# A hybrid decoder trunk: block attention with its transposes two heads back, the gated branch at even heads, weight rests one turn ahead

## The chip, the cores and the metric

One core of a Trainium2 chip runs the whole program. The metric is the time of one execution in microseconds on the device. The engines are TensorE (PE), VectorE (DVE), ScalarE (ACT), GpSimd (POOL) and SyncE (SP). Each works through its own program in order, and waits on semaphores for the others.

## What is computed

Two layers of a decoder trunk on 256 tokens of width 1024, float32. Each layer has a mixer of three branches, a cross-attention and a feed-forward part (dense in the first layer, 8 experts in the second). The part that matters here is the mixer's first two branches:

```python
y_a = moba_attention(q_m, k_m, v_m) @ w_up_moba[l]      # 8 heads of 64, causal, one block of 256
y_s = gelu(s5_ssm(u_s, ...))
glu_a, glu_b = split(y_s @ ssm_w_glu[l], 2)
y_b = glu_a * sigmoid(glu_b)
merged = sigmoid(gate_a) * y_a + sigmoid(gate_b) * y_b + sigmoid(gate_c) * y_c
```

With 256 tokens and blocks of 256 there is no past block, so `moba_attention` is causal softmax attention for each head.

## The kernel before

Tokens lie in two tiles of 128 partitions. The program is written by hand for every engine: each engine's block runs once over the layers, and the order of the work is the order of the Python code there. Products with precision beyond one pass use a split of both operands in a high part and a rest; ScalarE copies the high part of a weight group (`unit_split_hi`, L988), VectorE subtracts it (`unit_split_lo`, L1519), and `split_out` (L2409, L2410, L2413) multiplies low by high, high by high and high by low.

The attention stage of a layer mixes two kinds of work on TensorE. Its loop `for s in range(MH + 2)` does in turn s: the scores of head s (`m_scores`, L2587 and L2588), one half of a gated product of the second branch (`glu_half`, 12 products of 512 columns), the transposes of head s-1 (`m_tr`, L2597) and the output of head s-2 (`m_out`, L2608 to L2610). Two halves make one gated product, four products a stage. Behind the loop `up(U_UPM, ...)` projects the attention's output with the same `split_out` lines, on `m_hi` and `m_lo`.

For each head VectorE adds the causal mask and takes the row maxima (`moba_max`, L1765 to L1768), ScalarE takes exp (`moba_exp`, L1144 and L1146), VectorE divides by the row sums (`moba_norm`, L1774 to L1776), TensorE transposes, and ScalarE copies the transposed weights out of PSUM (`moba_pT`, L1154). For each gated product ScalarE takes tanh (`glu_tanh`, L1164), and VectorE works the branch out (`glu_branch`, L1782, L1785, L1786); the next gated product waits for its first instruction, which frees bank 0. For each pair of heads ScalarE copies the output's high part (`moba_oT`, L1158) and VectorE takes the rest (`moba_lo`, L1756). In between VectorE makes eight weight rests (L1519) of the next units.

VectorE's order is:

```python
moba_max(0)
for h in range(MH):
    if h + 1 < MH: moba_max(h + 1)
    moba_norm(h)
    if h % 2 == 1: glu_branch(h // 2)
    unit_split_lo(...)                       # one weight rest
    if h >= 3 and h % 2 == 1: moba_lo((h - 3) // 2)
moba_lo(MH // 2 - 1)
```

The probability buffers `mp_` are two, used by heads in turn, and the maxima, negated maxima and sums (`mx`, `nm`, `rs`) two columns for each. Behind the stage ScalarE goes on with the first taps of a convolution (`first_taps`, L1191), VectorE with the other taps (L1822) and `moba_branch` (L1833), which takes the projection.

## Time and profile before

| | us |
|---|---|
| three runs: median (lowest, highest) | 1891.79 (1882.14, 1892.0) |
| the profiled execution, its own time | 1885.03 |
| its span, first to last instruction | 1883.3 |
| TensorE busy | 1787.7 (95%) |
| VectorE busy | 1394.2 (74%) |
| ScalarE busy | 1044.9 (55%) |
| mean granted TensorE clock | 0.982 |
| attention stage, first layer | 222.0 to 266.4 |
| attention stage, second layer | 844.9 to 889.3 |

A stage is counted from its first scores to the start of the projection behind it. A granted clock of 1 is 2.4 GHz, of 0.5 is 1.2 GHz. Matmul records overlap, so a wait of TensorE is read from the brackets of a row, which give the idle time before it and what ended it.

### The profile page before, as it was taken

The numbers are of one execution on the slowest core, as the hardware profiler recorded it, in microseconds if no ns is written. First come the engines' busy times: TensorE is split into PE (matmuls) and PEld (weight loads), VectorE is DVE, ScalarE is ACT, GpSimd is POOL, SyncE is SP. The second block draws the span as 40 slices with busy tenths as digits, with TensorE's granted clock in tenths as the row PEclk, the third lists the DMA queues.
The fourth block names the chain that finished last, engine by engine and source line by source line (L and its number), as shares of the span: only waits on it lengthen the run. The fifth ranks groups of instructions, "written<-read, shape, count | busy, mean of one in ns | idle before, by whom it ended". The sixth has DMA issues, their size and how long they took to land.

```text
span 1883.3 us, 23760 instructions
## 1 busy us (share of the span) xinstructions
PE 1787.7 (95%) x9559; PEld 1421.6 (75%) x9559; DVE 1394.2 (74%) x1742; ACT 1044.9 (55%) x1208; POOL 171.9 (9%) x229
## 2 busy tenths in 40 slices
PE   7999999998999999999999889999999999999995
PEld 5787766576888788776657678787878787878784
DVE  5688678445555478867844478989898989989895
ACT  4234555345444422455523657767676767777773
POOL 8420002010000324000200010000000000000010
PEclk9999999999999999999999989999999999999998
DMA  7334431066552433543204469999999999999992
GB/s 248 135 135 155 158 111 69 1 247 236 176 200 89 155 131 135 179 164 105 90 1 163 174 252 390 379 389 361 389 359 389 362 389 360 390 358 390 347 391 84
DMA packets 204572, 434.93 MB, mean 231 GB/s; under 512 B 6888, under 2 KB 45936, under 8 KB 204464
## 3 DMA queue, kind: packets, MB, share of 16 engines
q1 hardware_dynamic: 196464, 414.20, 60.8%
q0 software_dynamic: 5136, 17.01, 2.5%
q10 hardware_dynamic: 2864, 2.23, 0.4%
q8 instruction: 73, 1.20, 0.3%
q14 instruction: 35, 0.29, 0.0%
HBM read 422.93 MB, written 10.49 MB: 230 GB/s over the span
## 4 chain that ended last, share of the span: by engine, by line
PE 79%; DVE 11%; ACT 6%; issue 3%; DMA 1%; ACTq 0%; POOL 0%; DVEq 0%; SPq 0%
PE bank L2855 14%; PE bank L2857 14%; PE bank L2856 14%; PE bank L2467 4%; DVE split_e L1525 3%; PE bank L2487 3%; PE bank L2491 3%; PE bank L2488 3%; PE bank L2409 2%; PE bank L2386 2%; PE bank L2413 2%; PE bank L2410 2%; PE bank L2393 2%; PE bank L2658 1%; DVE ring_r L1519 1%
## 5 line engine op out<-in xcount | busy, mean ns | idle before, releaser
L1525 DVE TENSOR_TENSOR split_e<-ring,split_e 128x2048 fp32r<-128x2048 f32 x264 | 600.3, 2288 | 51.0 <-ACT split_e L999 50.8
L999 ACT ACTIVATE split_e<-ring 128x2048 fp32r<-128x2048 f32 x264 | 503.8, 1919 | 160.7 <-PE bank L2857 157.1
L2855 PE MATMUL bank<-split_e,fx_e 128*128 128x512 f32 x704 | 278.8, 396 | 2.0 <-DVE fx_e L2246 2.0
L2857 PE MATMUL bank<-split_e,fx_e 128*128 128x512 f32 x704 | 274.7, 390 | 0.0
L2856 PE MATMUL bank<-split_e,fx_e 128*128 128x512 f32 x704 | 274.2, 389 | 0.0
L2855 PEld LDWEIGHTS bank<-split_e,fx_e 128*128 128x128 f32 x704 | 132.2, 188 | 28.2 <-DVE fx_e L2246 2.2
L2857 PEld LDWEIGHTS bank<-split_e,fx_e 128*128 128x128 f32 x704 | 132.1, 188 | 28.2
L2856 PEld LDWEIGHTS bank<-split_e,fx_e 128*128 128x128 f32 x704 | 132.4, 188 | 26.2
L2855 PE MATMUL bank<-split_e,f_actT_e 128*128 128x512 f32 x352 | 138.7, 394 | 9.2 <-DVE f_actT_e L2254 9.2
L2857 PE MATMUL bank<-split_e,f_actT_e 128*128 128x512 f32 x352 | 137.1, 389 | 0.0
L2856 PE MATMUL bank<-split_e,f_actT_e 128*128 128x512 f32 x352 | 137.1, 389 | 0.0
L988 ACT ACTIVATE ring_r<-ring 128x1024 fp32r<-128x1024 f32 x71 | 73.5, 1056 | 71.4 <-PE bank L2488 57.0
L1519 DVE TENSOR_TENSOR ring_r<-ring,ring_r 128x1024 fp32r<-128x1024 f32 x71 | 86.7, 1251 | 29.7 <-ACT ring_r L988 29.4
L2855 PEld LDWEIGHTS bank<-split_e,f_actT_e 128*128 128x128 f32 x352 | 66.1, 188 | 26.1 <-DVE f_actT_e L2254 12.8
L2467 PE MATMUL bank<-hT,ring 128*128 128x256 f32 x384 | 84.5, 381 | 0.0
L2467 PEld LDWEIGHTS bank<-hT,ring 128*128 128x128 f32 x384 | 72.5, 190 | 10.3
L2857 PEld LDWEIGHTS bank<-split_e,f_actT_e 128*128 128x128 f32 x352 | 66.1, 188 | 13.9
L2856 PEld LDWEIGHTS bank<-split_e,f_actT_e 128*128 128x128 f32 x352 | 66.1, 188 | 13.3
L2855 PE MATMUL bank<-split_mix,fx 128*128 128x512 f32 x168 | 66.5, 396 | 1.7 <-DVE phase L2189 1.7
L2857 PE MATMUL bank<-split_mix,fx 128*128 128x512 f32 x168 | 65.5, 390 | 0.0
L2856 PE MATMUL bank<-split_mix,fx 128*128 128x512 f32 x168 | 65.4, 389 | 0.0
L988 ACT ACTIVATE phase_r<-ring 128x1024 fp32r<-128x1024 f32 x34 | 35.7, 1057 | 46.4 <-PE bank L2488 46.4
(598 smaller groups left out, 3404.8 us busy)
## 6 DMA issues: line engine op xcount, KB each, us to landing
ring<-in_moe_w_gate SPq DMA_DIRECT2D x40, 2048.0 KB, 11.5
ring<-in_moe_w_up SPq DMA_DIRECT2D x40, 2048.0 KB, 11.5
ring<-in_moe_w_down SPq DMA_DIRECT2D x40, 2048.0 KB, 11.5
ring<-in_w_in SPq DMA_DIRECT2D x28, 2048.0 KB, 8.0
ring<-in_ffn_w_gate SPq DMA_DIRECT2D x11, 1024.0 KB, 5.5
ring<-in_ffn_w_up SPq DMA_DIRECT2D x11, 1024.0 KB, 8.0
ring<-in_ffn_w_down SPq DMA_DIRECT2D x11, 1024.0 KB, 8.8
ring<-in_ssm_w_glu SPq DMA_DIRECT2D x8, 1024.0 KB, 6.2
```

Source lines behind the costliest of these rows:

```text
L988: nc.scalar.activation(unit_hi(l, m), unit_raw(j, i), ACT.Copy).then_inc(split_hi, 1)
L999: nc.scalar.activation(split_e[j % NBUF][:, HI, :], ring[:, s * PIECE + i * HGRP:s * PIECE + (i + 1) * HGRP], ACT.Copy).then_inc(split_hi, 1)
L1519: V.tensor_tensor(unit_lo(j, i), unit_raw(j, i), unit_hi(l, m).bitcast(F32), ALU.subtract).then_inc(split_lo, 1)
L1525: V.tensor_tensor(split_e[j % NBUF][:, LO, :], ring[:, s * PIECE + i * HGRP:s * PIECE + (i + 1) * HGRP], split_e[j % NBUF][:, HI, :].bitca ...
L2386: last = mm(B[banks[m // 2]][:, (m % 2) * SEQ:(m % 2 + 1) * SEQ], w[:, k, m * P:(m + 1) * P], src[:, k, :], start=k == 0, stop=k == KD - 1)
L2467: last = mm(B[t][:, (m % 2) * SEQ:(m % 2 + 1) * SEQ], w[:, k, m * P:(m + 1) * P], hT[:, k, :], start=k == 0, stop=k == KD - 1)
L2487: mm(bank[:, :], h_lo[:, k, at], hi, start=k == 0, stop=False)
L2488: freed = mm(bank[:, :], h_hi(k)[:, at], hi, start=False, stop=False)
L2491: last = mm(bank[:, :], h_hi(k)[:, at], lo, start=False, stop=k == KD - 1)
L2855: mm(bank, a[HI], w[HI], start=first, stop=False)
L2856: mm(bank, a[HI], w[LO], start=False, stop=False)
L2857: return mm(bank, a[LO], w[HI], start=False, stop=last_one)
```

## The change

The three engines' programs of the attention stage are rewritten:

- TensorE's loop has one more turn. The transposes in turn s are those of head s-2, the output is that of head s-3. Scores and gated halves stay where they were.
- `mp_` has a third buffer, heads use them in turn by `h % 3`, and the maxima and sums have columns of their own (`m_mx`, `m_nm`, `m_rs`).
- ScalarE's copies of transposed weights follow: head s-2 in turn s, the output's high part at even turns from 4.
- VectorE takes the maxima two heads ahead, does the gated branch at even heads h, right behind the normalisation of head h, and has one weight rest between the first two maxima, with the others one turn ahead. `moba_lo` comes at even h from 4, the last two behind the loop.

```diff
--- before.py
+++ after.py
@@ -253,6 +253,8 @@
         glu_t = [rm.take(512) for _ in range(2)]
         glu_y = [rm.take(512) for _ in range(2)]
         gl_tmp = [rm.take(512) for _ in range(2)]
+        mp_.append(rm.take(3 * P))
+        m_mx, m_nm, m_rs = (st[:, 32 + 8 * i:38 + 8 * i] for i in range(3))
 
 
         rg = Region(phase, PH)
@@ -1139,12 +1141,12 @@
                 def moba_exp(h):
                     n = MH * l + h
                     act.wait_ge(ms_neg, n + 1)
-                    p = mp_[h % 2]
-                    o = 2 * (h % 2)
-                    nc.scalar.activation(p[:, 0:P], p[:, 0:P], ACT.Exp, bias=nm[:, o:o + 1], scale=MD ** -0.5,
-                                         accum_out=rs[:, o:o + 1])
-                    nc.scalar.activation(p[:, P:3 * P], p[:, P:3 * P], ACT.Exp, bias=nm[:, o + 1:o + 2],
-                                         scale=MD ** -0.5, accum_out=rs[:, o + 1:o + 2]).then_inc(ms_exp, 1)
+                    p = mp_[h % 3]
+                    o = 2 * (h % 3)
+                    nc.scalar.activation(p[:, 0:P], p[:, 0:P], ACT.Exp, bias=m_nm[:, o:o + 1], scale=MD ** -0.5,
+                                         accum_out=m_rs[:, o:o + 1])
+                    nc.scalar.activation(p[:, P:3 * P], p[:, P:3 * P], ACT.Exp, bias=m_nm[:, o + 1:o + 2],
+                                         scale=MD ** -0.5, accum_out=m_rs[:, o + 1:o + 2]).then_inc(ms_exp, 1)
 
                 def moba_pT(h):
                     n = MH * l + h
@@ -1163,19 +1165,19 @@
                         act.wait_ge(glu_used, 4 * l + i - 1)
                     nc.scalar.activation(glu_t[i % 2], B[1][:, :], ACT.Tanh, scale=0.5).then_inc(glu_th, 1)
 
-                for s in range(MH + 2):
+                for s in range(MH + 3):
                     if s < MH:
                         moba_exp(s)
                     if 2 <= s <= MH and s % 2 == 0:
                         glu_tanh(s // 2 - 1)
                     if 5 <= s <= 8:
                         unit_split_hi(l, U_UPM, [s - 5])
-                    if 1 <= s <= MH:
-                        moba_pT(s - 1)
+                    if 2 <= s <= MH + 1:
+                        moba_pT(s - 2)
                     if s < 2:
                         unit_split_hi(l, U_GLU + 1, [2 + s])
-                    if s >= 3 and s % 2 == 1:
-                        moba_oT((s - 3) // 2)
+                    if s >= 4 and s % 2 == 0:
+                        moba_oT((s - 4) // 2)
 
                 def keys_copy(b):
                     act.wait_ge(xk_ps, 6 * l + b + 1)
@@ -1758,22 +1760,24 @@
 
                 def moba_max(h):
                     n = MH * l + h
-                    p, o = mp_[h % 2], 2 * (h % 2)
+                    p, o = mp_[h % 3], 2 * (h % 3)
                     dve.wait_ge(ms_ready, n + 1)
-                    if n >= 2:
-                        dve.wait_ge(ms_tr, n - 1)
+                    if h >= 3:
+                        dve.wait_ge(ms_tr, n - 2)
+                    elif l > 0:
+                        dve.wait_ge(ms_tr, MH * l)
                     link(V.tensor_tensor(p, B[2 + h % 2][:, 0:3 * P], causal[:, :], ALU.add))
-                    V.tensor_reduce(mx[:, o:o + 1], p[:, 0:P], AX.X, ALU.max)
-                    link(V.tensor_reduce(mx[:, o + 1:o + 2], p[:, P:3 * P], AX.X, ALU.max))
-                    V.tensor_scalar(nm[:, o:o + 2], mx[:, o:o + 2], -MD ** -0.5, None, ALU.mult).then_inc(ms_neg, 1)
+                    V.tensor_reduce(m_mx[:, o:o + 1], p[:, 0:P], AX.X, ALU.max)
+                    link(V.tensor_reduce(m_mx[:, o + 1:o + 2], p[:, P:3 * P], AX.X, ALU.max))
+                    V.tensor_scalar(m_nm[:, o:o + 2], m_mx[:, o:o + 2], -MD ** -0.5, None, ALU.mult).then_inc(ms_neg, 1)
 
                 def moba_norm(h):
                     n = MH * l + h
-                    p, o = mp_[h % 2], 2 * (h % 2)
+                    p, o = mp_[h % 3], 2 * (h % 3)
                     dve.wait_ge(ms_exp, n + 1)
-                    link(V.reciprocal(rs[:, o:o + 2], rs[:, o:o + 2]))
-                    V.tensor_scalar(p[:, 0:P], p[:, 0:P], rs[:, o:o + 1], None, ALU.mult)
-                    V.tensor_scalar(p[:, P:3 * P], p[:, P:3 * P], rs[:, o + 1:o + 2], None, ALU.mult).then_inc(ms_norm, 1)
+                    link(V.reciprocal(m_rs[:, o:o + 2], m_rs[:, o:o + 2]))
+                    V.tensor_scalar(p[:, 0:P], p[:, 0:P], m_rs[:, o:o + 1], None, ALU.mult)
+                    V.tensor_scalar(p[:, P:3 * P], p[:, P:3 * P], m_rs[:, o + 1:o + 2], None, ALU.mult).then_inc(ms_norm, 1)
 
 
                 def glu_branch(i):
@@ -1789,19 +1793,22 @@
                     dve.wait_ge(consts, 4)
                 dve.wait_ge(mtr_ready, 4 * (l + 1))
                 moba_max(0)
+                unit_split_lo(l, U_GLU + 1, [0])
+                moba_max(1)
                 for h in range(MH):
-                    if h + 1 < MH:
-                        moba_max(h + 1)
+                    if h + 2 < MH:
+                        moba_max(h + 2)
                     moba_norm(h)
-                    if h % 2 == 1:
+                    if h % 2 == 0:
                         glu_branch(h // 2)
-                    if h < 4:
-                        unit_split_lo(l, U_GLU + 1, [h])
-                    if 4 <= h:
-                        unit_split_lo(l, U_UPM, [h - 4])
-                    if h >= 3 and h % 2 == 1:
-                        moba_lo((h - 3) // 2)
-                moba_lo(MH // 2 - 1)
+                    if h < 3:
+                        unit_split_lo(l, U_GLU + 1, [h + 1])
+                    elif h < 7:
+                        unit_split_lo(l, U_UPM, [h - 3])
+                    if h >= 4 and h % 2 == 0:
+                        moba_lo((h - 4) // 2)
+                for j in range(MH // 2 - 2, MH // 2):
+                    moba_lo(j)
 
                 ab4 = ab.rearrange("p (t c h) -> p t c h", t=NT, c=2)
                 z4 = gate_z.rearrange("p (t h) -> p t h", t=NT)
@@ -2594,7 +2601,7 @@
                     if h >= 2:
                         pe.wait_ge(ms_pT, n - 1)
                     for b in range(3):
-                        last = tr(B[4 + h % 2][:, b * P:(b + 1) * P], mp_[h % 2][:, b * P:(b + 1) * P], ident[:, :])
+                        last = tr(B[4 + h % 2][:, b * P:(b + 1) * P], mp_[h % 3][:, b * P:(b + 1) * P], ident[:, :])
                     last.then_inc(ms_tr, 1)
 
                 def m_out(h):
@@ -2622,15 +2629,15 @@
                     if half == 1:
                         last.then_inc(glu_ps, 1)
 
-                for s in range(MH + 2):
+                for s in range(MH + 3):
                     if s < MH:
                         m_scores(s)
                     if 1 <= s <= MH:
                         glu_half((s - 1) // 2, (s - 1) % 2)
-                    if 1 <= s <= MH:
-                        m_tr(s - 1)
-                    if s >= 2:
-                        m_out(s - 2)
+                    if 2 <= s <= MH + 1:
+                        m_tr(s - 2)
+                    if s >= 3:
+                        m_out(s - 3)
 
                 def up(j, src, n, src_ready, turns=range(4)):
                     for i in turns:
```

**VectorE, from the first gated branch to the next normalisation** (L1782 to L1786 are the branch, L1519 a weight rest, L1765 to L1768 the maximum, L1774 to L1776 the normalisation). Before:

```order
L1782 SCALAR_TENSOR_TENSOR phase<-phase,bank 128x512
L1785 SCALAR_TENSOR_TENSOR phase<-gates,phase 128x512
L1786 TENSOR_SCALAR qk<-phase 128x512
L1519 TENSOR_TENSOR ring_r<-ring,ring_r 128x1024
L1765 TENSOR_TENSOR phase<-bank,causal 128x384
L1766 TENSOR_REDUCE st<-phase 128x1
L1767 TENSOR_REDUCE st<-phase 128x1
L1768 TENSOR_SCALAR st<-st 128x2
L1774 RECIPROCAL st<-st 128x2
L1775 TENSOR_SCALAR phase<-phase,st 128x128
L1776 TENSOR_SCALAR phase<-phase,st 128x256
```

With the change:

```order
L1786 SCALAR_TENSOR_TENSOR phase<-phase,bank 128x512
L1789 SCALAR_TENSOR_TENSOR phase<-gates,phase 128x512
L1790 TENSOR_SCALAR qk<-phase 128x512
L1521 TENSOR_TENSOR ring_r<-ring,ring_r 128x1024
L1769 TENSOR_TENSOR phase<-bank,causal 128x384
L1770 TENSOR_REDUCE st<-phase 128x1
L1771 TENSOR_REDUCE st<-phase 128x1
L1772 TENSOR_SCALAR st<-st 128x2
L1778 RECIPROCAL st<-st 128x2
L1779 TENSOR_SCALAR phase<-phase,st 128x128
L1780 TENSOR_SCALAR phase<-phase,st 128x256
```

The rows are the same but for line numbers; before, the last three normalise head 2, now head 1.

**VectorE, the end of the stage, in the last gated branch.** Before:

```order
L1774 RECIPROCAL st<-st 128x2
L1775 TENSOR_SCALAR phase<-phase,st 128x128
L1776 TENSOR_SCALAR phase<-phase,st 128x256
L1782 SCALAR_TENSOR_TENSOR phase<-phase,bank 128x512
L1785 SCALAR_TENSOR_TENSOR phase<-gates,phase 128x512
L1786 TENSOR_SCALAR qk<-phase 128x512
L1519 TENSOR_TENSOR ring_r<-ring,ring_r 128x1024
L1756 TENSOR_TENSOR m_lo<-bank,m_hi 128x256 x2
L1810 TENSOR_TENSOR st<-st,small_bc 128x4 x2
```

With the change:

```order
L1786 SCALAR_TENSOR_TENSOR phase<-phase,bank 128x512
L1789 SCALAR_TENSOR_TENSOR phase<-gates,phase 128x512
L1790 TENSOR_SCALAR qk<-phase 128x512
L1521 TENSOR_TENSOR ring_r<-ring,ring_r 128x1024
L1758 TENSOR_TENSOR m_lo<-bank,m_hi 128x256
L1778 RECIPROCAL st<-st 128x2
L1779 TENSOR_SCALAR phase<-phase,st 128x128
L1780 TENSOR_SCALAR phase<-phase,st 128x256
L1758 TENSOR_TENSOR m_lo<-bank,m_hi 128x256 x2
L1817 TENSOR_TENSOR st<-st,small_bc 128x4 x2
```

The normalisation of head 7 has moved from ahead of the branch to behind it and its weight rest. An L1756 that followed the third branch now stands ahead of that normalisation; the last two L1756 stay last.

**TensorE, the end of the stage, from the last gated product on** (L2597 are transposes, L2608 to L2610 an output; L2604 and L2615 to L2617 with the change). Before:

```order
L2413 MATMUL bank<-ring_r,y_hi 128x512
L2597 MATMUL bank<-ident,phase 128x128 x3
L2608 MATMUL bank<-phase,v_tok 64x128
L2609 MATMUL bank<-phase,v_tok 64x128
L2610 MATMUL bank<-phase,v_tok 64x128
L2608 MATMUL bank<-phase,v_tok 64x128
L2609 MATMUL bank<-phase,v_tok 64x128
L2610 MATMUL bank<-phase,v_tok 64x128
L2409 MATMUL bank<-ring_r,m_lo 128x512
```

With the change:

```order
L2420 MATMUL bank<-ring_r,y_hi 128x512
L2604 MATMUL bank<-ident,phase 128x128 x3
L2615 MATMUL bank<-phase,v_tok 64x128
L2616 MATMUL bank<-phase,v_tok 64x128
L2617 MATMUL bank<-phase,v_tok 64x128
L2604 MATMUL bank<-ident,phase 128x128 x3
L2615 MATMUL bank<-phase,v_tok 64x128
L2616 MATMUL bank<-phase,v_tok 64x128
L2617 MATMUL bank<-phase,v_tok 64x128
L2615 MATMUL bank<-phase,v_tok 64x128
L2616 MATMUL bank<-phase,v_tok 64x128
L2617 MATMUL bank<-phase,v_tok 64x128
```

One output (of head 5) stands between the last gated product's transposes and those of head 7, and two outputs behind them, ahead of the projection.

## Rows read from the trace of the kernel before

**Rows 1.** The page's head and the shares of its chain by engine

```profile
span 1883.3 us, 23760 instructions
...
PE 79%; DVE 11%; ACT 6%; issue 3%; DMA 1%; ACTq 0%; POOL 0%; DVEq 0%; SPq 0%
```

**Rows 2.** Windows of the stage: us, busy PE, PEld, DVE, ACT, POOL, clock, DMA, GB/s

```profile
222.00:266.40 44.40, 39.71 (x201) 28.86 (x201) 31.71 (x78) 21.75 (x55) 1.17 (x2) 1.00 0.27 94
844.90:889.30 44.40, 39.67 (x200) 28.83 (x200) 31.69 (x78) 21.81 (x56) 1.17 (x2) 1.00 0.27 95
```

**Rows 3.** Timeline, TensorE: start us, us, engine, line, operation [idle before, releaser]

```profile
226.48 0.55 PE L2597 MATMUL bank<-ident,phase 128*128 128x128 f32 x3 [0.56 <-DVE phase L1776]
...
227.81 0.50 PE L2409 MATMUL bank<-ring_r,y_lo 128*128 128x512 f32 x1
...
236.65 0.55 PE L2597 MATMUL bank<-ident,phase 128*128 128x128 f32 x3 [0.86 <-DVE phase L1776]
...
247.95 0.55 PE L2597 MATMUL bank<-ident,phase 128*128 128x128 f32 x3 [1.19 <-DVE phase L1776]
...
259.25 0.55 PE L2597 MATMUL bank<-ident,phase 128*128 128x128 f32 x3 [1.19 <-DVE phase L1776]
```

**Rows 4.** Timeline, VectorE, a gated branch and what follows it, layer 0

```profile
231.50 0.69 DVE L1782 SCALAR_TENSOR_TENSOR phase<-phase,bank 128x512 f32<-128x512 f32 x1 [1.53 <-ACT phase L1164]
...
233.41 1.22 DVE L1519 TENSOR_TENSOR ring_r<-ring,ring_r 128x1024 fp32r<-128x1024 f32 x1
234.55 0.55 DVE L1765 TENSOR_TENSOR phase<-bank,causal 128x384 f32<-128x384 f32 x1
...
235.86 0.16 DVE L1774 RECIPROCAL st<-st 128x2 f32<-128x2 f32 x1
...
245.52 0.42 DVE L1756 TENSOR_TENSOR m_lo<-bank,m_hi 128x256 fp32r<-128x256 f32 x1
```

**Rows 5.** Timeline, VectorE, the last gated branch of the stage

```profile
264.23 0.69 DVE L1782 SCALAR_TENSOR_TENSOR phase<-phase,bank 128x512 f32<-128x512 f32 x1 [1.80 <-ACT phase L1164]
...
266.14 1.23 DVE L1519 TENSOR_TENSOR ring_r<-ring,ring_r 128x1024 fp32r<-128x1024 f32 x1
267.28 0.75 DVE L1756 TENSOR_TENSOR m_lo<-bank,m_hi 128x256 fp32r<-128x256 f32 x2
```

**Rows 6.** Timeline, TensorE, the end of the stage

```profile
263.41 0.49 PE L2597 MATMUL bank<-ident,phase 128*128 128x128 f32 x3
263.82 0.43 PE L2608 MATMUL bank<-phase,v_tok 128*64 128x128 f32 x2
...
265.58 0.43 PE L2608 MATMUL bank<-phase,v_tok 128*64 128x128 f32 x2 [0.88 <-ACT phase L1154]
...
266.38 0.50 PE L2409 MATMUL bank<-ring_r,m_lo 128*128 128x512 f32 x1
```

**Rows 7.** Timeline, ScalarE, the end of the stage

```profile
265.04 0.48 ACT L1154 ACTIVATE phase<-bank 128x384 f32<-128x384 f32 x1
266.48 0.39 ACT L1158 ACTIVATE m_hi<-bank 128x256 fp32r<-128x256 f32 x1 [0.96 <-PE bank L2610]
```

**Rows 8.** Chain that ended last, in order of time, behind the stage: start us, us, what

```profile
266.76 3.30 ACT phase L1191 x8
...
276.70 3.26 DVE phase L1822 x8
```

**Rows 9.** Timeline, TensorE, and windows of 1 us with the granted clock

```profile
287.99 5.40 PE L2672 MATMUL bank<-ring,ones 128*128 128x512 f32 x8 [2.73 <-ACT ring L1220]
...
289.00:290.00 1.00, 1.00 (x3) 0.44 (x2) 1.00 (x3) 1.00 (x3) 0.00 (x0) 0.71 0.00 0
290.00:291.00 1.00, 1.00 (x2) 0.34 (x1) 1.00 (x4) 0.98 (x2) 0.00 (x0) 0.50 0.00 0
291.00:292.00 1.00, 1.00 (x3) 0.43 (x2) 0.96 (x3) 0.99 (x3) 0.00 (x0) 0.50 0.00 0
292.00:293.00 1.00, 1.00 (x3) 0.47 (x2) 1.00 (x3) 1.00 (x3) 0.00 (x0) 0.59 0.00 0
```

## The prediction

> **What bounds the kernel now.** I read the page's head and chain first: a span of 1883.3 us, 79% of its chain on TensorE, only 11% on VectorE [rows 1]. The change is confined to the attention stage of the two layers. The windows of that stage show 44.4 us in each, TensorE busy for 39.7 of them, VectorE for 31.7 and ScalarE for 21.8, at the full granted clock [rows 2]. So no engine is full there: the loss is in hand-overs, and the order of waits decides. The two windows agree to 0.05 us of work, so I work the first layer out and count it twice.
>
> TensorE's timeline shows the hand-overs. It waits for the normalised weights of a head (released by VectorE's L1776) before the transposes of every second turn: 0.56, 0.86, 1.19 and 1.19 us [rows 3]. In the other turns it does not wait. Together that is 3.80 us a layer, and what the change could aim at.
>
> VectorE's timeline shows why every second turn. The gated branch starts when tanh is there (231.50). It holds VectorE to 233.41, the weight rest (L1519) to 234.55, the next head's mask and maximum to 235.86, and then the normalisation starts [rows 4]. The transposes start at 236.65 [rows 3]. From branch to transposes that is 1.91 + 1.14 + 1.31 + 0.79 = 5.15 us of VectorE's own in-order work. None of it is a wait for exp, and none a wait for another head's buffer. The 1.19 of the later turns is 0.33 more than 0.86: there the rest L1756 stands in the same row of work (its record alone is 0.42) [rows 3, 4].
>
> **The change, part by part.** A third probability buffer, their own statistics columns, and the altered waits of the maximum cost nothing by themselves: the same instructions run, and the buffers lie in space that is free at that time. What they could give is nothing either: the maximum never waited for a free buffer in the rows above.
>
> *TensorE transposes two heads back.* The transposes of head s-2 now stand where those of head s-1 stood. VectorE's program shifted along with them: between a gated branch and the transposes that wait for it there is still branch, weight rest, maximum, normalisation, only with a lower head number in the last. The order fences show it. So the 5.15 us stay, and with them the 0.86 waits. The extra head in flight is slack against exp, and exp is not what is late.
>
> *The start.* The first transposes leave the second turn: their wait of 0.56 goes, and they themselves (0.41, from 263.41 to 263.82 [rows 6]) move behind the second half of the gated product, which started at 227.81 [rows 3]. The first tanh, branch and everything chained to it come 0.56 + 0.41 = 0.97 us earlier. VectorE is ready for that: its rest, three maxima and normalisation take about 5.7 us by rows 4 from the first maximum, and the tanh comes after that. Gain: 0.97.
>
> *The L1756 rests come later.* The first of them leaves the second branch's row and goes to the third's, the second goes from the third to the last. So the wait behind the second branch falls from 1.19 to 0.86 [rows 3]: 0.33 gained. The third keeps its 1.19.
>
> *The weight rests one turn ahead.* The first now stands between the first two maxima. It delays the second maximum by 1.14, but its exp isn't needed before head 1 is normalised a turn later. Behind each gated branch there still stands exactly one rest. Cost and gain: nothing; should exp 1 be late after all, up to 1.14.
>
> *The end.* Here the shift has its price. Before, head 7 was normalised ahead of the last gated branch; its transposes and the output of head 6 ran at once (263.41, 263.82), the output of head 7 at 265.58 after ScalarE's copy of 265.04, and the next projection began at 266.38 [rows 6, 7]. That is 2.15 us behind the start of the last branch (264.23) [rows 5]. Now head 7's normalisation stands behind that branch, its weight rest and one L1756: 1.91 + 1.14 [rows 5] + 0.33, then 0.79 from normalisation to transposes [rows 3, 4], so the transposes start 4.17 behind the branch. Then they take 0.41, and the outputs of heads 6 and 7 0.80 each (265.58 to 266.38 [rows 6]); ScalarE's copy fits beside the first of these. The projection begins at 4.17 + 0.41 + 0.80 + 0.80 = 6.18. Loss: 6.18 - 2.15 = 4.03 us. TensorE stands idle for some 3.8 of it, from its output of head 5 (0.39 behind the branch's start) to 4.17.
>
> Is this loss covered by what follows? The chain behind the stage goes on with ScalarE's L1191 at 266.76, which stands in its program right behind the copy of head 7's output (266.48) [rows 7, 8]; that copy moves by the same 4.03. VectorE's next long piece, L1822 [rows 8], comes after a projection that moves by the same too. No engine has a start of its own there, so nothing is hidden.
>
> Sum for a layer: 4.03 - 0.97 - 0.33 = 2.73; for two 5.5 us.
>
> *TensorE's clock.* Behind a wait of 2.73 us the granted clock of this kernel fell to 0.71, 0.50, 0.50 and 0.59 in four successive microseconds, to its lower level (1.2 GHz) and back [rows 9]: 0.29 + 0.50 + 0.50 + 0.41 = 1.70 us of full-speed work lost. The stage itself, with waits of at most 1.19, kept 1.00 [rows 2, 3]. The new gap of 3.8 us is longer than the one of rows 9, so I expect a fall in each layer. If it lies inside the gap it costs nothing, if it lies on the transposes, outputs and projection, 1.70. I take the middle, 0.85 a layer, 1.7 us in all. The ends are 0 and 3.4. The Trainium skill (TensorE: Matmul & The Clock Gate, "Part 1: The HAM clock gate") says that TensorE drops to 1.2 GHz once it has been idle and gets 2.4 GHz back once it has been busy again. By that rule a fall is due in each layer, and the sum could be up to 5.5 + 3.4 = 8.9 (an estimate); by the stage's own rows, without a fall, it would be 5.5. Rows 9 agree with the rule, which speaks against this change.
>
> Forecast: 5.5 + 1.7 = 7.2 us slower. The profiled execution took 1885.03 by its own time, which gives 1892.2. But the three runs shown have their median at 1891.79 and their lowest at 1882.14, so executions of this kernel scatter by 10 us. The mean of all four is 1887.7; on it the changed kernel stands at 1895. About 0.5% (9.4 us) is what a measurement of this kernel can tell from no change, so the forecast is "no change", on the slow side.
>
> **Rivals.**
> *A, slower beyond 0.5%: TensorE stays at its lower clock.* Place: from the new gap through transposes and outputs (short bursts with little work) into the projection. If one fall follows another there, each at its 1.70 [rows 9], a layer loses 3.4 instead of 0.85, and the change 5.5 + 6.8 = 12.3 us: 1900 on the same mean (1897.3 on the profiled execution). It decides from the point where the second fall begins before the projection has run. For it: the gap is longer than in rows 9 and thin work follows. Against: in rows 9 the clock came back while work went on. The Trainium skill's rule above bears A out if those short bursts leave TensorE idle in its sense; no row shows that either way. Chance 0.16.
> *B, the pipeline does what its name says.* All waits of rows 3 vanish and the end is hidden: 3.80 a layer, 7.6 us, 1880 (1877.4 on the profiled execution). Against: the row of VectorE work between branch and transposes is the same by the order. Chance 0.08.
> *C, the end is taken up by the stage behind.* Then only 0.97 + 0.33 count: 2.6 us faster, 1885 (1882.4). For it: VectorE is busy there and waits little. Against: the chain starts that stage on ScalarE right behind the moved copy [rows 8]. Chance 0.10.
>
> **How the numbers follow.** Forecast 0.66, A 0.16, B 0.08, C 0.10. The range runs from C's 1885 to A's 1900, widened for the scatter of a median by 2 to 3 us, and leaves B and part of A out: 1883 to 1903. Slower by over 0.5%: three quarters of A (0.12), and a fifth of the forecast, whose 7.2 lies 2.2 below the bound (0.14), together 0.26. Faster by over 0.5%: half of B, helped by scatter, 0.04. The rest, 0.70, is no change.
>
> **What would show it.** In the changed profile each stage should show, on TensorE, no wait before the first transposes, then some 1.3 us before those of head 1 (the output that stood in this turn is gone, so TensorE is earlier there, while VectorE's 5.15 is the same), 0.86 before head 3, 1.19 before head 5, and a new wait of 3.7 to 3.8 before head 7, released by VectorE's normalisation (now L1780). The projection should begin 6.2 us behind the last branch, not 2.15, and the stage last 2.7 us longer at full clock, up to 6 us with falls. A lower clock should appear in the first microseconds around that wait. The forecast is wrong if the waits of heads 1, 3 and 5 vanish (B), if L1191 does not move against the last branch (C), or if the clock is below full for over 4 us in a layer (A).

## The result, and the profile after

The changed kernel takes 1889.63 us (median of 20 runs, 1887.14 to 1894.69), the kernel before 1884.8 us (20 runs, 1879.42 to 1892.0). The ratio is 1.0026, with a 95% interval of 1.0017 to 1.0035: the change makes the kernel slower by 4.9 us, between 3.2 and 6.6.

The page of the changed kernel, its head and the shares of its chain:

```profile
span 1887.1 us, 23759 instructions
...
PE 75%; DVE 14%; ACT 6%; issue 3%; DMA 1%; ACTq 0%; POOL 0%; DVEq 0%; SPq 0%
```

Against [rows 1] the span is 3.8 us longer, and 4% of the chain moved from TensorE to the others. The windows of the two stages, first scores to the projection, in the columns of [rows 2]:

```profile
223.20:271.10 47.90, 40.50 (x201) 29.56 (x201) 32.94 (x79) 21.84 (x55) 1.17 (x2) 0.97 0.33 124
848.00:895.90 47.90, 40.49 (x201) 29.57 (x201) 32.95 (x79) 21.88 (x55) 1.17 (x2) 0.97 0.35 123
```

A stage takes 47.9 us where it took 44.4 [rows 2]: 3.5 us more for the same instructions, and its mean clock is 0.97 where it was 1.00. TensorE's timeline, with the waits in brackets:

```profile
223.18 0.50 PE L2594 MATMUL bank<-phase 64*128 64x128 f32 x4 [0.98 <-ACT phase L1136]
...
230.81 0.38 PE L2604 MATMUL bank<-ident,phase 128*128 128x128 f32 x2
...
232.28 0.50 PE L2416 MATMUL bank<-ring_r,y_lo 128*128 128x512 f32 x1 [0.23 <-DVE phase L1786]
...
236.69 0.55 PE L2604 MATMUL bank<-ident,phase 128*128 128x128 f32 x3 [1.39 <-DVE phase L1780]
...
247.66 0.55 PE L2604 MATMUL bank<-ident,phase 128*128 128x128 f32 x3 [0.86 <-DVE phase L1780]
...
258.97 0.55 PE L2604 MATMUL bank<-ident,phase 128*128 128x128 f32 x3 [1.20 <-DVE phase L1780]
...
263.54 0.43 PE L2615 MATMUL bank<-phase,v_tok 128*64 128x128 f32 x2
...
268.13 0.90 PE L2604 MATMUL bank<-ident,phase 128*128 128x128 f32 x3 [3.72 <-DVE phase L1780]
268.96 0.69 PE L2615 MATMUL bank<-phase,v_tok 128*64 128x128 f32 x2
...
271.08 0.72 PE L2416 MATMUL bank<-ring_r,m_lo 128*128 128x512 f32 x1
```

These rows answer to [rows 3, 6]. The wait of 0.56 before the first transposes is gone (230.81, no bracket). Those of every second turn are there: 1.39, 0.86 and 1.20, and a small one of 0.23 before a gated product. New is the wait of 3.72 before the last transposes, which VectorE's L1780 ends, the normalisation of head 7. From those transposes (268.13) to the projection (271.08) it is 2.95 us. VectorE's side, first and last gated branch:

```profile
231.53 0.69 DVE L1786 SCALAR_TENSOR_TENSOR phase<-phase,bank 128x512 f32<-128x512 f32 x1 [1.49 <-ACT phase L1166]
...
263.95 0.69 DVE L1786 SCALAR_TENSOR_TENSOR phase<-phase,bank 128x512 f32<-128x512 f32 x1 [1.80 <-ACT phase L1166]
...
265.86 1.23 DVE L1521 TENSOR_TENSOR ring_r<-ring,ring_r 128x1024 fp32r<-128x1024 f32 x1
267.00 0.42 DVE L1758 TENSOR_TENSOR m_lo<-bank,m_hi 128x256 fp32r<-128x256 f32 x1
267.34 0.16 DVE L1778 RECIPROCAL st<-st 128x2 f32<-128x2 f32 x1
```

The first branch starts 8.35 us behind the first scores (223.18), where it was 9.50 (222.00 to 231.50). Behind the last one (263.95) stand the weight rest, an L1758 and only then the normalisation (267.34); the transposes start 4.18 us behind the branch. ScalarE, in answer to [rows 7, 8]:

```profile
271.19 0.38 ACT L1160 ACTIVATE m_hi<-bank 128x256 fp32r<-128x256 f32 x1 [1.63 <-PE bank L2617]
271.47 3.29 ACT L1193 ACTIVATE phase<-phase,params 128x256 f32<-128x256 f32 x8
```

It starts on L1193 (before: L1191) 0.28 us behind its copy of the last output, as before, and the chain goes on from there. The windows of 1 us around the last transposes:

```profile
267.00:268.00 1.00, 0.00 (x0) 0.00 (x0) 0.96 (x6) 0.00 (x0) 0.00 (x0) 1.00 0.97 369
268.00:269.00 1.00, 0.87 (x4) 0.54 (x4) 0.41 (x2) 0.00 (x0) 0.00 (x0) 0.58 1.06 408
269.00:270.00 1.00, 1.00 (x8) 1.00 (x9) 0.00 (x0) 0.49 (x1) 0.00 (x0) 0.50 1.02 389
270.00:271.00 1.00, 1.00 (x9) 0.75 (x5) 0.00 (x0) 0.00 (x0) 0.00 (x0) 0.50 0.85 330
271.00:272.00 1.00, 1.00 (x4) 0.82 (x4) 0.39 (x2) 0.81 (x3) 0.00 (x0) 0.71 0.13 49
272.00:273.00 1.00, 1.00 (x6) 0.81 (x5) 0.34 (x4) 1.00 (x3) 0.00 (x0) 1.00 0.00 0
```

In the gap TensorE's clock was still granted in full; at 268 it fell to the lower level and came back before 272. Adding up what each microsecond lacks to 1.00, that loses 0.42 + 0.50 + 0.50 + 0.29 = 1.71 us of full-speed work, the size of the fall in [rows 9]. The fall of [rows 9] itself, at 289, has no counterpart here. The wait that came ahead of it is there:

```profile
292.69 3.70 PE L2679 MATMUL bank<-ring,ones 128*128 128x512 f32 x8 [2.63 <-ACT ring L1222]
```

but the products behind it start at full clock:

```profile
293.00:294.00 1.00, 1.00 (x3) 0.38 (x2) 0.96 (x4) 1.00 (x3) 0.00 (x0) 1.00 0.00 0
```

The first products of the loop behind them, in the first layer, before and after:

```profile
306.35 1.37 PE L2719 MATMUL bank<-uT,ring 64*64 64x64 f32 x32 [0.43 <-POOL ring L876]
...
309.42 1.36 PE L2726 MATMUL bank<-uT,ring 64*64 64x64 f32 x32 [0.49 <-POOL ring L878]
```

From these sums of squares (287.99 in [rows 9], 292.69 here) to the loop (L2719 before, L2726 after) the profile of before has 18.4 and 18.2 us in its two layers, that of after 16.7 in both. So the profiled executions differ by 2 x 3.52 in the stages, less 1.63 and 1.47 behind them: 3.9, where the span differs by 3.8. Elsewhere they differ too, but the differences cancel: the changed one reaches its first stage 1.2 us later and is 1.3 us faster behind the second layer's loop.

### The profile page after: what moved, and what is told of

The parts are those of the page before. It is cut to its first block, busy times and chain, and to the rows that moved or that the text cites. A ratio compares the mean times of both kernels' runs of the same rounds, so it can differ in the third digit from the quotient of the medians.

```text
span 1887.1 us, 23759 instructions
## 1 busy us (share of the span) xinstructions
PE 1785.5 (95%) x9559; PEld 1421.8 (75%) x9559; DVE 1393.9 (74%) x1742; ACT 1045.1 (55%) x1208; POOL 172.5 (9%) x229
## 4 chain that ended last, share of the span: by engine, by line
PE 75%; DVE 14%; ACT 6%; issue 3%; DMA 1%; ACTq 0%; POOL 0%; DVEq 0%; SPq 0%
PE bank L2862 14%; PE bank L2864 14%; PE bank L2863 14%; PE bank L2474 4%; DVE split_e L1527 3%; PE bank L2494 3%; PE bank L2498 3%; PE bank L2495 3%; PE bank L2416 2%; PE bank L2420 2%; PE bank L2417 2%; PE bank L2400 2%; PE bank L2393 1%; DVE ring_r L1521 1%; PE bank L2665 1%
## 5 line engine op out<-in xcount | busy, mean ns | idle before, releaser
L1521 DVE TENSOR_TENSOR ring_r<-ring,ring_r 128x1024 fp32r<-128x1024 f32 x71 | 86.8, 1251 | 29.9 <-ACT ring_r L990 29.5
```

Of the source, the lines that this page charges most:

```text
L1521: V.tensor_tensor(unit_lo(j, i), unit_raw(j, i), unit_hi(l, m).bitcast(F32), ALU.subtract).then_inc(split_lo, 1)
```

## Experiments

Ratios are to the kernel before on the same chip, with 95% intervals. "Stage" is the time from the first scores to the projection in a profile; where one number stands, both layers agree within 0.1 us.

### The last normalisation alone

In the kernel before, only head 7's normalisation is put behind the last branch and its weight rest:

```diff
-                    moba_norm(h)
+                    if h < MH - 1:
+                        moba_norm(h)
                     if h % 2 == 1:
                         glu_branch(h // 2)
...
                         unit_split_lo(l, U_UPM, [h - 4])
+                    if h == MH - 1:
+                        moba_norm(h)
```

> The kernel before with one part of the change alone: head 7 is normalised behind the last gated branch and its weight rest. The stage is the time from the first scores to the start of the projection, 44.4 us before and 47.9 with the change. Order theory: the projection starts 5.85 us behind the last branch instead of 2.15, so the stage takes 44.4 + 3.7 = 48.1 us, and up to 0.9 more with a lower clock on the outputs: 48.1 to 49.0. Clock theory (a fall of the clock taken in the gap of the stage is the one that otherwise comes behind it): the clock falls once in the gap, the fall some 20 us behind the stage is gone, that part is 1.6 us shorter, and the whole is slower by 2 x (3.7 + 0.9 - 1.6) = 6 us. Rival to it (falls come at their own times): the later fall stays, and the whole is 7.4 to 9.2 us slower. Rival to the order theory (VectorE catches up elsewhere): stage under 45 us and no change in all.

Measured: 1893.32 us against 1884.06, ratio 1.0055 (1.0037 to 1.0073), 9.3 us slower. Stage 49.0. TensorE at its end:

```profile
269.58 0.90 PE L2600 MATMUL bank<-ident,phase 128*128 128x128 f32 x3 [4.51 <-DVE phase L1776]
...
272.53 0.80 PE L2412 MATMUL bank<-ring_r,m_lo 128*128 128x512 f32 x1
```

The gap is 4.51 us, the projection starts 2.95 behind the transposes, as with the change. So the one moved step costs 4.6 us a layer, fall of the clock included, more than the 3.5 of the whole change. In the first layer the fall in the gap was a double one (3.4 us of work lost), which made the way from the projection to the sums of squares 0.5 us longer, and the later fall came too (18.4 us from the sums of squares to the loop); in the second it stayed away (16.7). In microseconds the interval is 7.0 to 13.8: it leaves out the 6 us of a fall that is always moved and takes in the 7.4 to 9.2 of falls that come at their own times.

### The last normalisation ahead again

The changed kernel, with heads 6 and 7 both normalised ahead of the last branch:

```diff
+                    if h == MH - 2:
+                        moba_lo(1)
-                    moba_norm(h)
+                    if h < MH - 1:
+                        moba_norm(h)
+                    if h == MH - 2:
+                        moba_norm(h + 1)
                     if h % 2 == 0:
                         glu_branch(h // 2)
...
-                    if h >= 4 and h % 2 == 0:
-                        moba_lo((h - 4) // 2)
+                    if h == 4:
+                        moba_lo(0)
```

> The changed kernel, with head 7's normalisation and the L1756 kind of rest of heads 2 and 3 ahead of the last gated branch. Order theory: the gap of 3.7 us before the last transposes goes, the three waits of 1.4, 0.9 and 1.2 us stay, and the stage takes 43.8 us, 0.6 less than before and 4.1 less than with the change. No fall of the clock in the stage, and the one behind it is there again. In all 1.2 us faster than before (ratio 0.9994), which 5 rounds may not tell from no change, and some 6 us faster than the change. Rival (the transposes two heads back cost by themselves): stage over 45 us, slower than before.

Measured: 1.0004 (0.9989 to 1.0018), with the expected 0.9994 inside, median 1885.01. Stage 43.6, expected 43.8. Transposes of heads 6 and 7 and the projection:

```profile
262.41 0.49 PE L2609 MATMUL bank<-ident,phase 128*128 128x128 f32 x3
...
263.63 0.55 PE L2609 MATMUL bank<-ident,phase 128*128 128x128 f32 x3
...
266.04 0.50 PE L2421 MATMUL bank<-ring_r,m_lo 128*128 128x512 f32 x1
```

The gap is gone, the 1.40, 0.86 and 1.23 of the other turns are not. The end is the whole of the change's cost; what is left gains 0.8 us a layer in the stage, less than the ratio can tell. So the transposes two heads back cost nothing by themselves.

### The gap filled

The changed kernel with work that nobody reads, ahead of head 7's transposes. Its only use is to keep TensorE active:

```diff
+                    if s == MH + 1:
+                        for _ in range(5):
+                            mm(B[2][:, 0:3 * P], ident[:, :], causal[:, :], start=True, stop=True)
                     if 2 <= s <= MH + 1:
                         m_tr(s - 2)
```

> The changed kernel with five products of 384 columns (masks, result never read) on TensorE in the gap before the last transposes, 3.2 us of work where it idled for 3.7. Order theory: the transposes start at the same time as with the change. Clock theory: the clock stays at 1.00 in the stage, the last transposes and outputs take 2.0 us instead of 2.95, the stage 47.0; but the fall of the kernel before, some 20 us behind the stage, is back and costs 1.6 there, so the whole is 5.2 to 6.3 us slower than the kernel before. Rival (falls come at their own times): the stage is 47.0 and nothing is lost behind it, the whole 3 us slower than the kernel before. If the filler delays the transposes, the stage is 47.9 or more.

Measured: 1.0020 (1.0008 to 1.0031), 3.8 us slower than before. Stage 46.9. The window of the first layer's stage, then TensorE at its end:

```profile
226.15:273.01 46.86, 42.88 (x211) 30.65 (x211) 32.93 (x79) 21.84 (x55) 1.17 (x2) 1.00 0.34 121
...
267.29 3.49 PE L2639 MATMUL bank<-causal,ident 128*128 128x384 f32 x10
271.08 0.55 PE L2604 MATMUL bank<-ident,phase 128*128 128x128 f32 x3 [0.30 <-DVE phase L1780]
...
273.01 0.50 PE L2416 MATMUL bank<-ring_r,m_lo 128*128 128x512 f32 x1
```

The transposes still wait for VectorE (0.30), so their time is set by its order, not by TensorE. From there to the projection it is 1.93 us instead of 2.95: the fall of the clock costs 1.02 us of a stage. This stage is 2.5 us longer than before at full clock: that is the order's price alone. Behind it, the later fall was absent in the first layer and there in the second. The whole doesn't decide between the two: its interval is 1.5 to 5.8 us and holds both the rival's 3 and part of the 5.2 to 6.3 of a fall that always comes back.

### The weight rests back

The changed kernel with all eight weight rests at the loop index they had before:

```diff
                 moba_max(0)
-                unit_split_lo(l, U_GLU + 1, [0])
                 moba_max(1)
...
-                    if h < 3:
-                        unit_split_lo(l, U_GLU + 1, [h + 1])
-                    elif h < 7:
-                        unit_split_lo(l, U_UPM, [h - 3])
+                    if h < 4:
+                        unit_split_lo(l, U_GLU + 1, [h])
+                    else:
+                        unit_split_lo(l, U_UPM, [h - 4])
```

> The changed kernel with the weight rests where they stood before: none between the first two maxima, all one turn later. My theory: behind each gated branch there is still one rest, so nothing moves on TensorE: stage 47.9 us (within 0.2), the whole as the changed kernel, 4.9 us slower than before (ratio 1.0026). Rival (the rest between the first maxima costs its 1.14 at the start): 1.1 us less a layer, 2.3 in all.

Measured: 1.0073 (1.0055 to 1.0092), 1896.93 us: against the changed kernel's 1.0026 some 9 us more. Both theories fell. Stage 52.6 and 49.4. TensorE in the middle of the stage:

```profile
244.90 0.50 PE L2415 MATMUL bank<-merged_hi,y_lo 128*128 128x512 f32 x1 [0.28 <-DVE ring_r L1521]
...
248.00 0.50 PE L2415 MATMUL bank<-merged_hi,y_lo 128*128 128x512 f32 x1 [2.14 <-DVE ring_r L1521]
...
248.80 0.58 PE L2603 MATMUL bank<-ident,phase 128*128 128x128 f32 x3
```

Inside the third gated product TensorE waits 0.28 and 2.14 us for weight rests (L1521): this product is the first that uses unit `U_GLU + 1`, and with VectorE's loop index now two turns behind TensorE's, the rests of that unit come too late. In the second layer, with the same two waits, the stage is 1.5 us longer than with the change (2.4 us of new waits, while the 0.86 before head 3's transposes is gone). In the first layer the clock fell behind them too (249 to 256, 3.4 us of work lost), and it is 4.7 us longer. The stages make 6.1 of the 9 us. The later fall came in both layers of this profile (18.4 us from the sums of squares to the loop) and adds up to 3.3 more against the changed kernel's profile above, where it came in neither. So "one turn ahead" is no ornament: it only restores the distance that the shift takes away, and it was needed.

### The normalisations ahead of every branch

The changed kernel's buffers and TensorE order, with VectorE's loop written for pairs:

```diff
+                for i in range(MH // 2):
+                    h = 2 * i
+                    if h + 2 < MH:
+                        moba_max(h + 2)
+                    if i >= 2:
+                        moba_lo(i - 2)
+                    moba_norm(h)
+                    moba_norm(h + 1)
+                    glu_branch(i)
+                    for g in (h + 1, h + 2):
+                        if g == h + 2 and h + 3 < MH:
+                            moba_max(h + 3)
+                        if g < 4:
+                            unit_split_lo(l, U_GLU + 1, [g])
+                        elif g < MH:
+                            unit_split_lo(l, U_UPM, [g - 4])
```

and on ScalarE `unit_split_hi(l, U_UPM, [s - 5])` ahead of `moba_exp(s)`.

> The changed kernel with VectorE's order rewritten: both normalisations of a pair and the L1756 kind of rest stand ahead of the gated branch, and ScalarE copies the high parts of the next unit's weights ahead of exp in turns 5 to 8. Order theory: what delays the transposes is the branch, a weight rest and a maximum that stand ahead of a normalisation in VectorE's row, and the third buffer makes it possible to put the normalisation first. Then no transposes wait for VectorE and the stage takes 39.3 us (before 44.4, changed 47.9). The whole is 10.2 us faster than before, ratio 0.9946. Rival (VectorE's total work is the limit, so another wait takes the place of those removed): stage over 42 us, less than 5 us faster.

Measured: 1874.85 us against 1885.11, ratio 0.9931 (0.9910 to 0.9953), 10 us by the medians and 13 by the ratio faster than before. The expected 0.9946 lies inside, the rival's "less than 5 us" (0.9973) outside. Windows of the stages, and VectorE around the first gated branch with the transposes that follow:

```profile
225.00:264.08 39.08, 38.85 (x201) 29.07 (x201) 31.70 (x78) 21.99 (x55) 1.17 (x2) 1.00 0.31 108
842.90:882.00 39.10, 38.87 (x201) 29.09 (x201) 31.76 (x78) 22.00 (x55) 1.17 (x2) 1.00 0.31 109
```

```profile
231.12 0.16 DVE L1778 RECIPROCAL st<-st 128x2 f32<-128x2 f32 x1
231.78 0.16 DVE L1778 RECIPROCAL st<-st 128x2 f32<-128x2 f32 x1
...
233.39 0.69 DVE L1786 SCALAR_TENSOR_TENSOR phase<-phase,bank 128x512 f32<-128x512 f32 x1 [0.86 <-ACT phase L1166]
...
235.30 1.23 DVE L1521 TENSOR_TENSOR ring_r<-ring,ring_r 128x1024 fp32r<-128x1024 f32 x1
236.44 0.55 DVE L1769 TENSOR_TENSOR phase<-bank,causal 128x384 f32<-128x384 f32 x1
...
236.99 0.49 PE L2608 MATMUL bank<-ident,phase 128*128 128x128 f32 x3
```

A stage takes 39.1 us, of which TensorE works 38.9. Behind the branch stand the weight rest and the maximum as ever, but two heads are normalised ahead of it (231.12 and 231.78), and the transposes (236.99) wait for nothing. VectorE's busy time is the 31.7 us of [rows 2]: its amount of work wasn't the limit, the place of the normalisation in its row was. The expectation says that the third buffer makes this order possible. No run tried it with two buffers, so what the third one is worth stays open.

With ScalarE's order left as in the changed kernel:

> The same, with ScalarE's order as in the changed kernel, where the copy of the high part comes behind exp and VectorE's weight rest waits for it. Order theory: two waits before transposes (1.0 and 0.3 us) remain, the stage takes 40.8 us, the whole is 7 us faster than before (0.9962), 3 us slower than its sister. Rival: the sisters are equal.

Measured: 0.9956 (0.9941 to 0.9971), stage 40.5, with one wait of 0.77 us left in the middle. The expected 0.9962 lies inside. The sisters differ in their stages by 1.4 us (1.5 was expected); in the whole their intervals overlap.

### The later gap filled

Four products that nobody reads stand in the wait ahead of the sums of squares, in the kernel before:

```diff
                 memory_keys(0, 2)
 
+                for _ in range(4):
+                    mm(B[7][:, 0:3 * P], ident[:, :], causal[:, :], start=True, stop=True)
```

> The kernel before with four products of 384 columns (masks, result never read) on TensorE in the wait of 2.7 us some 19 us behind the projection's start, ahead of the sums of squares. Nothing else moves: stage 44.4 us, and from its end to the sums of squares 21.6. If the clock falls behind that wait in every run and layer, the filler keeps it up and gives 2 x 1.6 = 3.3 us (ratio 0.9983); if the falls come at their own times in about half of the cases, as in the profiles so far, 1.6 us (0.9991); if filling does nothing to the clock, no change, and the profile shows 18.4 us from the sums of squares to the next loop instead of 16.7.

Measured: 0.9977 (0.9962 to 0.9991), 1881.6 us against 1885.11. The filler, the sums of squares and the window behind it (us, busy PE, PEld, DVE, ACT, POOL, clock):

```profile
286.60 2.74 PE L2671 MATMUL bank<-causal,ident 128*128 128x384 f32 x8
289.50 3.70 PE L2675 MATMUL bank<-ring,ones 128*128 128x512 f32 x8
...
289.00:293.00 4.00, 3.85 (x10) 1.63 (x9) 3.93 (x9) 3.97 (x7) 0.00 (x0) 1.00 0.02 4
```

The clock stays at 1.00 where [rows 9] had 0.71, 0.50, 0.50, 0.59, and the sums of squares to the loop take 16.7 us in both layers. Stage 44.4. The 0.9983 expected of a fall in every run and layer lies well inside the interval, the 0.9991 of a fall in half of them at its edge.

The mean granted clock of every run is on record, and the span times what it lacks to 1 is the full-speed work that the run lost. On average that is 32.3 us for the kernel before (63 runs) and 27.3 with the filler (12 runs): 5.0 less, give or take 1.3. Two falls of 1.7 make 3.4 of it. So the filler seems to have spared the kernel further falls elsewhere, which no run isolates.

The same in the changed kernel:

> The changed kernel with the same filler in the same later wait. If the change moved the fall of the clock from there into the stage for good (both layers of its profile show none behind), the filler finds nothing to save: 4.9 us slower than before, as the changed kernel (1.0026). If falls come at their own times and the changed kernel's profile was one draw, the filler gives 1.6 us: 3.2 us slower than before (1.0017).

Measured: 1.0020 (1.0005 to 1.0034). Both expected values, 1.0026 and 1.0017, lie inside: inconclusive. The work lost is 2.3 us less than the changed kernel's (give or take 2.2), which speaks weakly for falls that the filler could save.

### More profiles of the same kernels

Three more executions were profiled, two of the changed kernel and one of the kernel before, to see whether the missing later fall belongs to the change.

> The changed kernel, another profile. Moved for good: no fall behind the stage in either layer (16.7 us from the sums of squares to the next loop). Own times: 18.4 in some.

> The changed kernel, a third profile. As the second look: moved for good gives 16.7 us twice, own times gives 18.4 in some.

> The kernel before, another profile. If its falls behind the stage come in every run, 18.4 us from the sums of squares to the next loop in both layers; if at their own times, 16.7 in some.

Measured: 1891.9, 1890.1 and 1885.89 us. Of the changed kernel's second profile, a window in its first stage's end and one behind the stage:

```profile
269.00:270.00 1.00, 1.00 (x5) 0.67 (x5) 0.07 (x1) 0.33 (x1) 0.00 (x0) 0.50 1.04 406
...
293.00:294.00 1.00, 0.70 (x1) 0.50 (x2) 0.97 (x3) 1.00 (x3) 0.00 (x0) 0.50 0.00 0
```

This execution has both falls, and 18.1 and 18.4 us behind the sums of squares. Its third profile has 18.4 and 16.7, the second of the kernel before 18.4 and 18.1. So "moved for good" is wrong. In all profiles without filler at that place, the later fall came in 10 of 12 layers of kernels with no fall in the stage's end, and in 6 of 10 with one. These counts are too small to show that it comes less often behind a fall in the stage; both layers without it among the 12 are of kernels with the changed order on TensorE (the two runs above with the last normalisation ahead again and with the gap filled).

The work lost, as worked out above from the granted clock of each run, is 34.4 us on average for the changed kernel (20 runs) against 32.3 before (63 runs): 2.1 more, give or take 1.7. A new fall in each layer adds 3.4. If each only took the place of the later fall, the difference would be 0, which is outside; with half of the later falls missing it would be 1.7, which fits, but 3.4, with none missing, lies inside too.

### Both together

> The reordered kernel (normalisations ahead of the branch, 0.9931 of the kernel before) with the filler of four products in the later wait too. The two act at different places, so their gains add: stage 39.1 us, from the sums of squares to the next loop 16.7 instead of 18.4 in both layers, ratio 0.9931 x 0.9977 = 0.9908, some 17 us faster than before. Rival (the filler only moves the fall to a later place): ratio 0.993, with one more fall in the attention output behind it.

Measured: 1869.73 us against 1884.92, ratio 0.9916 (0.9901 to 0.9931), 15 us faster. Stage 39.0. The clock kept 1.00 from the stage to the loop in both layers (16.7 us). The interval holds the sum of the two gains, 0.9908, and just reaches the rival's 0.993 of a fall that only moves. Further on, some 135 us behind the start of a stage, the reordered kernel's profile lost 3.4 and 1.7 us of work in its two layers and this one's none and 5.1, no more in all, which doesn't bear the rival out. It is the fastest kernel of this study and beats both given ones.

## Why the prediction was right or wrong

The range (1883 to 1903) held the measured 1889.63, but the forecast was "no change", and the kernel is slower, by 3.2 to 6.6 us. The step that failed is the last one: a sum of 7.2 us slower was turned into "no change" because 0.5% (9.4 us) was taken for the least that a measurement could tell. It told 4.9 us. That the time lies in the range owes much to its width of 20 us. The mechanism was right: the last normalisation behind the branch is the cost, as taking it back (1.0004) and moving it alone (1.0055) show. Of the terms of the sum the clock's was mis-sized.

**The order of VectorE's row: right.** The 5.15 us from branch to transposes stayed (231.53 to 236.69 is 5.16), and the waits of 1.3, 0.86 and 1.19 came as 1.39, 0.86 and 1.20. Rival B had no basis in this order; the reordered kernel, where the waits before the transposes do vanish, needed another order.

**The start: right, a little more.** 0.97 was expected, 1.15 measured.

**The L1756 rests: right.** 1.19 became 0.86.

**The end: right.** 4.17 us from branch to transposes were expected, 4.18 measured. With the clock kept up the stage grew by 2.5 us, against 2.73 in the sum. Rival C is out: L1193 follows the moved copy at the same 0.28 us, and from the projection to the sums of squares it is 21.6 us before and after.

**The weight rests: wrong.** I called their shift free and idle. Undone it costs some 9 us, 6.1 of them in the stages. I had counted what stands behind a branch and not asked which gated product uses which unit. In the changed kernel the step does no more than keep an old distance, so the sum wasn't hurt.

**The clock: the term that was mis-sized.** I added 0.85 us a layer for a fall in the new gap. It came in every profile of the changed kernel and cost 1.02, less than the 1.71 us of full-speed work that it lost. But I treated it as an addition to the kernel's other falls. The sum should have asked what becomes of the fall of [rows 9], some 20 us on: in the changed kernel's three profiles it was missing in three of six layers, worth 1.6 us each, 0.8 on average. A layer then costs 2.5 + 1.0 - 0.8 = 2.7 and the change 5.4 us, inside the 3.2 to 6.6 measured; the 7.2 forecast is outside. The half rests on six layers; the work lost over all runs (2.1 us more, give or take 1.7) is in line with it, but would allow that none is missing. Why the fall is missing there, the runs left open.

**The measurement: the step that failed.** I took 0.5% as what could be told from no change, from three runs that scatter by 10 us. Twenty runs of each gave 0.26%, give or take 0.09%, though single runs of the kernel before scatter by 12.6 us: the scatter of single runs isn't the uncertainty of a median of twenty. Their median for the kernel before is also 1884.8, next to the profiled 1885.03 and not to the 1887.7 that I had moved the sum to. The sum on the profiled execution gave 1892.2, 2.6 above the measured 1889.63.

**Rival A**, a second fall following the first, came in one layer in six (3.4 us of work lost, in the third profile) and in one of the two layers of the first experiment. It exists, but is the exception, and was priced too high: the second half of it cost 0.8 us of time in the one and 0.5 in the other, behind the stage.

## What to carry to other kernels

A deeper pipeline between engines gains nothing while the late step stands behind other work in its own engine's row: first read what precedes it there, and move it. When a stage is shifted by a turn, look at its last turn (what used to hide the last item is gone) and at every producer whose deadline is counted in the other engine's turns. A new gap on TensorE can cost more than its length, since the work behind it can run at the lower clock: here 1.0 us on top of 3.7.

## What was not expected of the hardware

A fall of the granted clock lost 1.70 or 1.71 us of full-speed work, here and in [rows 9], or a multiple of it (3.41 the most common), whatever ran meanwhile; in all 14 profiles only the last stretch before the program's end differs. What it cost in time depended on the work under it: 1.0 us on short transposes and outputs, 1.5 to 1.6 on the products behind the sums of squares. Whether it came after a wait of 2.7 us differed between executions of one kernel (18.4 and 16.7 us behind the same wait). And work that nobody reads pays: 2.7 us of it in that wait made the kernel before 0.23% faster (0.09 to 0.38%); in its profile the clock stays at 1.00 there in both layers.
